# One decoder step on one core: levels two to six of the recurrent layer's matrix computed for the later half of each block only

## The reference, cut to what matters

```python
def step(S, inp):                       # one chunk of c tokens
    qb, kb, vb, fb = inp
    b = jnp.cumsum(fb, axis=2)
    inter = jnp.einsum('bhtk,bhkv->bhtv', qb * jnp.exp(b), S)
    diff = b[:, :, :, None, :] - b[:, :, None, :, :]
    decay = jnp.exp(jnp.where(causal[:, :, None], diff, -jnp.inf))
    att = jnp.einsum('bhtk,bhsk,bhtsk->bhts', qb, kb, decay)
    intra = jnp.einsum('bhts,bhsv->bhtv', att, vb)
    ...
```

## Time and profile before

| | |
|---|---|
| median of three runs | 1778.12 us (1776.62 to 1784.16) |
| the profiled execution | 1779.31 us, of it 1777.6 us between its first and last instruction |
| PE busy | 1323.7 us (74%) |
| PEld busy | 749.5 us (42%) |
| DVE busy | 727.5 us (41%) |
| ACT busy | 382.8 us (22%) |
| POOL busy | 173.1 us (10%) |
| mean granted TensorE clock | 0.868 of 2.4 GHz |
| masked copies L707 | 48, 35.1 us busy |
| level products L819 | 384 records (192 instructions), 52.6 us busy |

### The profile page before, as it was taken

The page is one execution under the profiler, slowest core; times in us unless marked ns, Lnnn a source line. Parts: engine busy times, 40 slices in busy tenths (PEclk is TensorE's granted clock), DMA queues, the critical chain, the costliest instruction groups (busy, mean ns, idle before and its releaser), DMA issues. The chain is left out here.

```text
span 1777.6 us, 28471 instructions
## 1 busy us (share of the span) xinstructions
PE 1323.7 (74%) x10955; PEld 749.5 (42%) x10955; DVE 727.5 (41%) x1726; ACT 382.8 (22%) x1038; POOL 173.1 (10%) x244
## 2 busy tenths in 40 slices
PE   4998988886793798908998745777666579199880
PEld 2445554544442455504444333444443235155440
DVE  4215565547535111132101186677767153411115
ACT  2023343334111111112001023333333211011111
POOL 1002232223002000020000010000000000200002
PEclk9999999987796799958998978888888789589995
DMA  5132243223601699940221179999998860279974
GB/s 193 48 124 68 93 131 113 79 96 109 220 21 63 252 367 360 360 153 16 95 98 48 54 268 354 357 357 362 354 358 344 331 227 1 101 279 355 344 224 159
DMA packets 133607, 352.61 MB, mean 198 GB/s; under 512 B 22220, under 2 KB 52095, under 8 KB 125280
## 3 DMA queue, kind: packets, MB, share of 16 engines
q1 hardware_dynamic: 117108, 320.32, 50.3%
q0 software_dynamic: 4992, 17.83, 2.9%
q10 hardware_dynamic: 11372, 12.62, 2.2%
HBM read 302.88 MB, written 47.84 MB: 197 GB/s over the span
## 5 line engine op out<-in xcount | busy, mean ns | idle before, releaser
L432 PE MATMUL bank<-wring,xT 128*128 128x512 f32 x768 | 353.1, 621 | 22.7 <-ACT gla_fin L552 16.1
L432 PEld LDWEIGHTS bank<-wring,xT 128*128 128x128 f32 x768 | 151.6, 200 | 211.4 <-issue 191.7
L2112 DVE STREAM_TRANSPOSE wring<-wring 128x1024 f32<-128x1024 f32 x128 | 154.0, 1225 | 54.3 <-DMA wring<-cache_k 52.9
L2002 PE MATMUL bank<-wring,sa_q 128*32 128x128 f32 x2048 | 89.0, 346 | 103.4 <-DVE sa_red L2121 96.0
L2002 PEld LDWEIGHTS bank<-wring,sa_q 128*32 128x32 f32 x2048 | 77.9, 141 | 112.3 <-issue 102.7
L799 PE MATMUL bank<-xT,wring 128*128 128x512 f32 x256 | 111.9, 595 | 0.0
L799 PEld LDWEIGHTS bank<-xT,wring 128*128 128x128 f32 x256 | 48.1, 190 | 59.2 <-issue 59.2
L707 DVE COPY_PREDICATED gla_att<-level_masks,bank 128x512 f32<-128x512 int32 x48 | 35.1, 731 | 91.6 <-PE bank L819 91.6
L819 PE MATMUL bank<-gla_qe,gla_ke 128*128 128x128 f32 x384 | 52.6, 296 | 4.7 <-DVE gla_att L707 4.7
L1764 PE MATMUL bank<-attn_q_xT,wring 128*128 128x512 f32 x128 | 55.7, 594 | 0.0
L1670 POOL COPY sa_q<-sa_q_rep 32x64 f32<-32x64 f32 x64 | 16.8, 262 | 377.6 <-PE bank L2002 237.6
(11 more groups left out here) (392 smaller groups left out, 2087.9 us busy)
## 6 DMA issues: line engine op xcount, KB each, us to landing
wring<-cache_k SPq DMA_DIRECT2D x128, 512.0 KB, 5.7
moe_wd<-moe_w_down SPq DMA_DIRECT2D x32, 1024.0 KB, 15.3
wring<-cache_v SPq DMA_DIRECT2D x64, 512.0 KB, 7.3
xT<-cache_v SPq DMA_DIRECT2D x64, 512.0 KB, 6.3
moe_wgu<-moe_w_gate SPq DMA_DIRECT2D x22, 1024.0 KB, 11.6
moe_wgu<-moe_w_up SPq DMA_DIRECT2D x22, 1024.0 KB, 13.3
wring<-a_w_in SPq DMA_DIRECT2D x16, 1024.0 KB, 9.0
slots_x<-gla_vm SPq DMA_DIRECT2D x27, 384.0 KB, 5.6
```

The lines of the kernel that those rows point to most:

```text
L432: last = nc.tensor.matmul(bank[:, :], xT[:, c, cols(t)], w[:, c, :], start=(c == 0), stop=(c == DC - 1))
L2002: last = nc.tensor.matmul(out.rearrange("p (r x) -> p r x", r=GROUP), Q[b % 2][:, h, i, :], keys.K[s % 2][:, :, at:at + QUAD], start=(i == ...
L2112: nc.vector.transpose(page, page).then_inc(keys_turned, 1)
```

## The change

`QE[1]` to `QE[5]` shrink to 256 columns: they hold only the later half of each block, packed, 64 columns for each chunk of 128 tokens. L697 writes them packed and reads as before. Their memsets at the start go. The products of levels 1 to 5 have 64 moving columns instead of 128, with the same 128 stationary columns; the bank then holds 4 x 64 columns. The copies of these levels take 128x256 elements out of the bank and write them, under the mask's later halves, with strides into `A`. Level 0 is left as it was, and so are `KE`, the exponentials and every wait.

```diff
-        QE = [sb(f"gla_qe{i}", [P, TOK if i == 0 else SEQ]) for i in range(NLEV)]
+        QE = [sb(f"gla_qe{i}", [P, TOK if i == 0 else SEQ // 2]) for i in range(NLEV)]
...
                 for i, lev in enumerate(LEVELS):
-                    nc.vector.memset(QE[i + 1][:, :], 0.0)
                     ch(nc.vector.memset(KE[i + 1][:, :], 0.0))
...
-                            nc.vector.tensor_tensor(blocks(QE[j][:, :], size)[:, :, up], blocks(q[h % 2][:, 0:SEQ], size)[:, :, up],
+                            nc.vector.tensor_tensor(blocks(QE[j][:, :], size // 2), blocks(q[h % 2][:, 0:SEQ], size)[:, :, up],
                                                     blocks(diff[j % 2][:, 0:SEQ], size)[:, :, up], ALU.mult).then_inc(q_lev, 1)
...
-                        nc.vector.copy_predicated(A[:, :, :], bcast(k.levelmask[:, i, :].bitcast(I32), 1, [P, PT, P]),
-                                                  k.ps[3 + i % 2][:, :].rearrange("p (c n) -> p c n", c=PT)).then_inc(att_taken, 1)
+                        if i == 0:
+                            kept, mask = A[:, :, :], bcast(k.levelmask[:, i, :].bitcast(I32), 1, [P, PT, P])
+                            src = k.ps[3][:, :].rearrange("p (c n) -> p c n", c=PT)
+                        else:
+                            size = LEVELS[i - 1]
+                            n, half = P // size, size // 2
+                            later = k.levelmask[:, i, :].bitcast(I32).rearrange("p (n r) -> p n r", r=size)[:, :, half:size]
+                            kept = A[:, :, :].rearrange("p c (n r) -> p c n r", r=size)[:, :, :, half:size]
+                            mask = bcast(later, 1, [P, PT, n, half])
+                            src = k.ps[3 + i % 2][:, 0:SEQ // 2].rearrange("p (c n r) -> p c n r", c=PT, r=half)
+                        nc.vector.copy_predicated(kept, mask, src).then_inc(att_taken, 1)
...
                         for c in range(PT):
-                            part = slice(c * P, (c + 1) * P)
-                            last = nc.tensor.matmul(k.ps[3 + i % 2][:, part], KE[i][:, part], QE[i][:, part], start=True, stop=True)
+                            n = P if i == 0 else P // 2
+                            part = slice(c * n, (c + 1) * n)
+                            last = nc.tensor.matmul(k.ps[3 + i % 2][:, part], KE[i][:, c * P:(c + 1) * P], QE[i][:, part], start=True, stop=True)
```

## The result

The changed kernel takes 1789.56 us in the median of nine runs (1787.31 to 1800.77), against 1780.17 for nine runs of the kernel before on the same chip (1774.25 to 1784.16). The ratio is 1.0062, 95% interval 1.0044 to 1.0080: slower by 0.6%. The forecast was 1778.0, within 1772 to 1786.

A forecast was written before the change was run, and what follows sets the result against it. A closed ring per head, with the matrix engine on it during the levels, was taken as the bound. 1779.31 - 0.8 (fills) - 2.3 (waits) + 3.0 (clock) = 1779.2, profiled 1.2 above the median: forecast 1778.0 us, range 1772 to 1786.

The forecast's parts named there:

- the clock term: Eighth head: the clock's rise to 2.4 GHz comes later, behind L834 or in L839; costs 3.0 us, between 0 and 5.
- a rival of 4.7 us: Seventh head: the clock's rise is delayed there too, 40 narrow records and L834 dearer; 4.7 us on top, 1782.7, chance 0.13.
- the other heads: Heads other than the eighth: levels begin at the full clock, so the clock costs 0 there.
- The load sets the pace of the products: Narrow products of the levels: loading 128 stationary columns sets the pace, so halving the moving columns saves 0.
- the moving-column rival: Levels of all heads: moving columns set the pace after all; 1.6 us a head faster, 1764.5 us, chance 0.05.
- A short copy: Masked copies of the five narrow levels: 0.465 us each instead of 0.731, bounds 0.425 and 0.731.
- One wait a head: Levels of the first six heads: the matrix engine's 0.27 us wait for a copy goes, 1.6 us together.
- The fills' wait at the start: First projections: with five fills gone, L642 is early enough for the second 32 products; 0.8 us go.
- the slower rival: Levels of every head: the clock falls inside them as the array streams less; 1804.5 us, chance 0.06.
- the signs: Profile marks for a right forecast: 16 loads in 1.87 us, shorter copies, no early stall, eighth head's clock 0.50 through L834.
- the term for the first six heads: First six heads: the clock stands at 1.00 by their levels, so its cost there is 0.
- the copy chain: Moving-column case, between levels: signals, copies and the end of a level add to 1.38 us instead of 2.05.

The follow-up runs named there:

- e2: Changed kernel with the 64 packed columns of the narrow products streamed twice in the seventh and eighth heads alone; 1775.64 us, ratio 0.9963 to the kernel before.
- e3: Changed kernel with the 64 packed columns of the narrow products streamed twice in the first six heads alone; 1790.35 us, ratio 1.0033 to the kernel before.
- e6: Changed kernel with eight of ten gate multiplications moved from ahead of the last head's copies into idle time of earlier heads; 1785.82 us, ratio 1.0037 to the kernel before.
- e5: Changed kernel with L839's products on 128 rows, 96 of them zeros, instead of 32; 1774.44 us, ratio 0.9966 to the kernel before.
- e10: Changed kernel with the gate multiplications moved to earlier heads and L839's products on 128 rows; 1776.91 us, ratio 0.9959 to the kernel before.
- e9: Changed kernel with four needless fills on the vector engine, so the seventh head is entered later; 1783.54 us, ratio 1.0001 to the kernel before.
- e11: Changed kernel with 16 moving columns instead of 64 in the narrow levels, output not the reference's; 1822.69 us, ratio 1.0220 to the kernel before.
- e12: Changed kernel with five zero fills of 128x512 put back on another tile; 1790.32 us, ratio 1.0045 to the kernel before.
- e1: Changed kernel with the 64 packed columns of the narrow products streamed twice in all heads; 1775.01 us, ratio 0.9958 to the kernel before.
- e4: Kernel before with the short strided copies alone, products and fills as they were; 1776.11 us, ratio 0.9980 to the kernel before.

## Why the prediction was wrong

The step that failed is the clock term, "I take 3.0 us, between 0 (no delay) and 5", for the eighth head alone, with the seventh as a rival of 4.7 us and a chance of 0.13. Measured in the profiled execution the eighth head cost 6.4 us and the seventh 8.6. The mechanism was named, and e2 and e3 show it in just these two heads; its size and its place were wrong in two ways.

First, I let the clock rise "behind L834 or in L839". L839 streams its 512 columns on 32 rows, and the clock stayed at 0.50 through it (changed kernel, e6) but rose in it with 128 rows (e5, e10). What the sum did price in the eighth head came out about as summed: the levels 1.6 us (1.6 to 2.0), L834 0.9 (0.8), L839 1.8 (up to 1.9). It took only a part of L839, and had no term for L844 to L851, 2.1 us.

Second, the sum took 0 for "the other heads", whose levels "begin at the full clock". The seventh's didn't, as the rival itself says: its first 3.2 us were at 0.50 before the change too, and it got the clock on its way. It had entered 3.6 us behind the fall; the changed kernel entered it 1.1 us behind one, with narrow products, and e9 shows that the later entry alone brings this head back to 15.2 us. The rival's 4.7 us were levels and L834, for which 4.2 were measured; L839 and what follows, 4.4 us, were missing there too.

The other steps held. The load sets the pace of the products (1.86 us for 16 loads at 64 columns, and at 16 columns in e11), so the moving-column rival was rightly low. A short copy takes 0.438 us against 0.465. One wait a head went, 2.2 us from the first to the seventh head against the 1.6 summed for these six. The fills' wait at the start is gone. The falling clock inside every head, the slower rival, didn't happen at 64 columns and did at 16.

Of the signs, two came otherwise than forecast. The third head began its transposes at 0.50 and had the clock only 1.8 us later, at 235.1, so it takes 14.3 us where the others take 13.4; this is 0.9 us that the term for the first six heads put at 0. And the clock of the eighth head wasn't at 0.50 throughout up to L834, but was up from 443.3 to 446.7, around the beginning of the stall. Three sums are off by a little and change nothing: 40 records at 0.1 us and L834 are 4.8 us, not 4.7, the slower rival adds up to 1804.7 with the 22 us it takes, not 1804.5, and the copy chain to 1.39 us, not 1.38. That the clock stands at 1.00 in all of the first six heads, shows for the fourth alone.

The missing terms could have been priced in part ahead of the result. The rows had L839's place at full clock, 1.98 us, and that records take about twice as long at 0.50; the bound of the clock term should have gone on to the last product of the head instead of ending in L839.

What stays open: what fixes the moment at which a head begins relative to the clock. All nine runs of the changed kernel were at 1787 us or above, but e3 and e12, with the same products in these two heads, have runs down to 1772 and 1780. Open too is whether the rows count in proportion or only as the sum of what streams.

## What to carry to other kernels

Before narrowing the moving operand of a product, see what sets its pace: if it is the load of the stationary operand, next to nothing is saved (0.07 us a head here), and the array has less to do. Where such a stretch is entered at the lower clock, price all that follows it at that clock until products on all rows have streamed for some time: here the rise came 1.9 to 3.4 us into 512 columns on 128 rows (e5, e10), and where these ran on 32 rows, 5.5 and 4.5 us into the 128-column products from L844 on (changed kernel, seventh and eighth head). Then look whether the elements can be saved on the side that reads the bank alone: keep the products wide, and make the copies short, as e1 and e4 do.

## What the runs showed of the hardware that was not expected

Products of 512 columns on 32 rows streamed for 3.7 us at a granted clock of 0.50 and didn't bring it up; padded with 96 rows of zeros, the same products did within 1.9 us in the eighth head (e5) and 2.7 us in the seventh (e10). Adding 2 us of needless work ahead of a head made a kernel 6 us faster (e9). Wide products got the clock back in either pattern of entry, 3.2 to 6.0 us behind the start of the transposes; narrow ones only in one, 3.7 and 3.8 us behind it (e9, e5), and otherwise, with L839 on 32 rows, after 22.6 to 22.9 us. Between 64 and 16 moving columns, with the loads unchanged, lies the step from a clock that stays at 2.4 GHz in the first six heads to one that falls (e11).
